# S5 output on TensorE as four 32-column sets side by side, with block 1's units and small steps in another order

## The reference, cut to what matters

```python
bu = jnp.einsum('blgh,gph->blgp', ug.astype(jnp.complex64), b_bar)
_, states = lax.associative_scan(combine, (a_seq, bu), axis=1)
y = jnp.einsum('blgp,ghp->blgh', states, c_mat).real + d.astype(f32) * ug
y = jax.nn.gelu(y.reshape(Bsz, L, S5_WIDTH))
y = y * jax.nn.sigmoid(y @ w_glu.astype(f32) + b_glu.astype(f32))
...
merged = g_s5 * (y_s5 @ w_br_s5[l]) + g_m * (y_m @ w_br_m[l])
x = x + merged @ w_out[l]
```

## Time and profile before

| | |
|---|---|
| median of 3 runs | 1433.69 us (1433.32 to 1433.8) |
| the profiled execution | 1439.07 us, of which the trace spans 1437.8 us |
| mean granted clock of TensorE | 0.949 of full speed |

### The profile page before, as it was taken

The page is one execution under the profiler, slowest core; times in us unless marked ns, Lnnn a source line. Parts: engine busy times, 40 slices in busy tenths (PEclk is TensorE's granted clock), DMA queues, the critical chain, the costliest instruction groups (busy, mean ns, idle before and its releaser), DMA issues. The chain is left out here.

```text
span 1437.8 us, 21155 instructions
## 1 busy us (share of the span) xinstructions
PE 1322.6 (92%) x8531; PEld 1204.6 (84%) x8537; DVE 897.0 (62%) x1291; ACT 590.5 (41%) x900; POOL 119.5 (8%) x152
## 2 busy tenths in 40 slices
PE   8988999999899999979987899999789898899996
PEld 5876788878589999869977799997779888799995
DVE  5957981125566777755476666666634585666666
ACT  2331111113355555543453554555411364554553
POOL 3890000003000000010000000010400000000000
PEclk9999899999999999999997999999887798999999
DMA  9434233427045556535502355565455202355561
GB/s 282 146 95 149 83 118 126 142 94 229 25 131 181 187 177 195 185 94 176 160 17 91 136 184 178 198 204 146 107 129 165 80 1 64 134 185 178 198 210 60
DMA packets 178590, 202.76 MB, mean 141 GB/s; under 512 B 21868, under 2 KB 163147, under 8 KB 178492
## 3 DMA queue, kind: packets, MB, share of 16 engines
q1 hardware_dynamic: 174939, 191.49, 42.0%
q0 software_dynamic: 3184, 9.77, 2.3%
q10 hardware_dynamic: 369, 0.13, 0.1%
HBM read 200.30 MB, written 1.08 MB: 140 GB/s over the span
## 5 line engine op out<-in xcount | busy, mean ns | idle before, releaser
L1317 DVE TENSOR_TENSOR w_parts<-raw,w_parts 128x1024 fp32r<-128x1024 f32 (+1 forms) x268 | 333.8, 1245 | 167.1 <-ACT w_parts L1306 159.6
L1306 ACT CAST w_parts<-raw 128x1024 fp32r<-128x1024 f32 (+1 forms) x268 | 279.3, 1042 | 337.6 <-PE ps L1600 103.3
L1600 PEld LDWEIGHTS ps<-hT_parts,w_parts 128*128 128x128 f32 x3024 | 366.6, 192 | 2.1
L1600 PE MATMUL ps<-hT_parts,w_parts 128*128 128x256 f32 x3024 | 367.6, 283 | 0.0
L1613 PE MATMUL ps<-w_parts,gT_parts 128*128 128x512 f32 x720 | 168.9, 390 | 0.0
L1613 PEld LDWEIGHTS ps<-w_parts,gT_parts 128*128 128x128 f32 x720 | 133.3, 188 | 26.4
L1366 PE MATMUL ps<-w_parts,hT_parts 128*128 128x256 f32 (+1 forms) x864 | 117.6, 303 | 16.7 <-DVE w_parts L1317 12.1
L1366 PEld LDWEIGHTS ps<-w_parts,hT_parts 128*128 128x128 f32 x864 | 116.2, 212 | 18.1 <-DVE w_parts L1317 12.5
L1364 PE MATMUL ps<-hT_parts,w_parts 128*128 128x256 f32 x912 | 120.8, 298 | 8.5 <-DVE w_parts L1317 4.5
L1364 PEld LDWEIGHTS ps<-hT_parts,w_parts 128*128 128x128 f32 x912 | 119.4, 207 | 10.0 <-issue 5.0
L451 PE MATMUL ps<-hT,ring 128*128 128x256 f32 x448 | 99.0, 380 | 1.0 <-DVE hT L310 1.0
(11 more groups left out here) (407 smaller groups left out, 1519.3 us busy)
## 6 DMA issues: line engine op xcount, KB each, us to landing
raw<-in_ffn_w_up SPq DMA_DIRECT2D x44, 1024.0 KB, 5.1
raw<-in_f_w_up SPq DMA_DIRECT2D x22, 1024.0 KB, 5.1
raw<-in_ffn_w_down SPq DMA_DIRECT2D x22, 1024.0 KB, 5.1
ring<-in_w_in SPq DMA_DIRECT2D x18, 1024.0 KB, 6.1
raw<-in_ev_w_in SPq DMA_DIRECT2D x15, 1024.0 KB, 5.4
raw<-in_f_w_down SPq DMA_DIRECT2D x11, 1024.0 KB, 4.9
ring<-in_x_wkv SPq DMA_DIRECT2D x8, 1024.0 KB, 5.5
ring<-in_w_out SPq DMA_DIRECT2D x4, 1024.0 KB, 5.1
```

The costliest lines, as they stand in the source:

```text
L1306: self.done(A, A.copy(high[:, c], self.raw[:, u % RAW, c]), self.s_hi)
L1317: self.done(V, V.tensor_tensor(low[:, c], self.raw[:, u % RAW, c], high[:, c].bitcast(F32), ALU.subtract), self.s_lo)
L1600: mm = T.matmul(self.ps[:, b, m * 256:m * 256 + 256], w[:, kk, m * P:(m + 1) * P], x[:, kk, :], start=kk == 0 and q == 0, stop=kk == KD - ...
```

## The change: what it does

1. `pe_s5_out` writes four tiles of 32 PSUM partitions in one bank. Pair m's weights are the 32 columns of `Cs` themselves at tile position (0, 32m). The products m = 0 to 3 use different columns of the array, and i = 1 (the imaginary part) adds to i = 0.
2. `CP` is gone, with its two clearings and 32 copies on DVE. PE waits for the scan's last addition (semaphore `x`) in place of the last copy (`cp`).
3. Units 8, 9 and 10 come one small step earlier: 8 ahead of the scores, 9 ahead of the turn, 10 ahead of the values, and no unit stands between the values and the first `pe_s5_in`.
4. The S5 steps and ym move among units 11 to 25, on PE and in step with it on ACT; on DVE the drain of ym moves from behind the second scan to behind the first.
5. The unit of `w_glu` becomes number 26 and the last values unit 27, and a unit of values stands between `w_glu` and the branch units.
6. Unit 32 no longer waits for the whole merged activation: its first half (j = 0) waits before each second k-block for the quarter that it reads.

```diff
@@ block1_memory
-        self.qkp, self.CP = p(18480, 8, SEQ + 3), [p(18480 + i * 512, 4, P) for i in range(2)]
+        self.qkp = p(18480, 8, SEQ + 3)
+        self.Cs = self.Bf
@@ early_units
-        u += [("T", wkv, D + c * 256, mT, KD, 256, 256) for c in range(4)]
+        values = [("T", wkv, D + c * 256, mT, KD, 256, 256) for c in range(4)]
+        u += values[0:3]
         u += [("F", I["s5_w_glu"][0], 0, self.yS, 4, 512, 256)]
+        u += values[3:4]
@@ pe_unit
-    def pe_unit(self, u):
+    def pe_unit(self, u, ready=None):
...
                 for kk in range(k):
+                    if ready is not None and j == 0 and kk % 2 == 0:
+                        T.wait_ge(*ready[kk // 2])
@@ pe_block1
-        T.wait_ge(*s5["merged"].at(4))
-        for u in range(32, 36):
+        self.pe_unit(32, [s5["merged"].at(i + 1) for i in range(4)])
+        for u in range(33, 36):
             self.pe_unit(u)
@@ pe_s5_out
-        T.wait_ge(*self.s5sem["cp"].next("T"))
+        T.wait_ge(*self.s5sem["x"].next("T"))
...
-                mm = T.matmul(self.ps[:, b, 0:256], self.CP[i][:, m, :], self.W5[5 + i][:, m, :],
-                              start=i == 0 and m == 0, stop=i == 1 and m == 3)
+                mm = T.matmul(self.ps[32 * m:32 * m + 32, b, 0:256], self.Cs[i][:, 4 * c4 + m, :], self.W5[5 + i][:, m, :],
+                              start=i == 0, stop=i == 1, tile_position=(0, 32 * m))
@@ act_block1 (the steps follow PE's order; the sigmoids of w_glu)
-        self.act_fill_unit(14)
         self.act_drain_gain(self.ym_fills, self.yM, "m_norm_g", kt=4)
+        self.act_fill_unit(14)
...
-            f = self.eu_fills[27][hh]
+            f = self.eu_fills[26][hh]
...
+        self.act_fill_unit(27)
@@ dve_block1
         self.dve_s5_scan(0)
+        self.dve_drain_gain(self.ym_fills, self.yM, "m_norm_g", kt=4)
         self.dve_s5_scan(1)
-        self.dve_drain_gain(self.ym_fills, self.yM, "m_norm_g", kt=4)
@@ dve_s5_scan
-            for i in range(2):
-                v1(v.memset(self.CP[i], 0.0))
...
-        v1(v.tensor_tensor(xi, xi, t1, ALU.add))
-        for i in range(2):
-            for m in range(4):
-                ins = v.tensor_copy(self.CP[i][:, m, 32 * m:32 * m + 32], self.Cs[i][:, 4 * c4 + m, :])
...
+        self.done(v, v.tensor_tensor(xi, xi, t1, ALU.add), s5["x"])
```

More of the change, by code:

```diff
@@ L495, in pe_block1 @@
         self.pe_mlstm_rows()
-        for u in (5, 6, 7):
+        for u in (5, 6, 7, 8):
             self.pe_unit(u)
         self.pe_mlstm_scores()
-        self.pe_unit(8)
+        self.pe_unit(9)
         self.pe_mlstm_turn()
@@ L502, in pe_block1 @@
         self.mem_fills = self.pe_transposes(self.MEM)
-        self.pe_unit(9)
+        self.pe_unit(10)
         self.pe_mlstm_values()
-        self.pe_unit(10)
         self.pe_wait_drained([self.eu_fills[5][0], self.eu_fills[6][0], self.bt_fills[1]])
         self.pe_s5_in(0)
-        self.pe_unit(11)
-        self.pe_unit(12)
+        for u in (11, 12, 13):
+            self.pe_unit(u)
         self.pe_s5_in(1)
-        self.pe_unit(13)
-        self.pe_s5_out(0)
-        self.pe_unit(14)
         T.wait_ge(*self.mls["h"].next("T"))
         self.ym_fills = self.pe_transposes(self.h8.rearrange("p (c h) d -> p c (h d)", c=2), kt=4)
+        self.pe_unit(14)
         self.pe_unit(15)
+        self.pe_s5_out(0)
+        self.pe_unit(16)
         self.pe_s5_in(2)
-        self.pe_unit(16)
-        self.pe_s5_out(1)
         self.pe_unit(17)
         self.pe_unit(18)
-        self.pe_s5_in(3)
+        self.pe_s5_out(1)
         self.pe_wait_drained(self.mem_fills[-2:])
         self.pe_unit(19)
+        self.pe_s5_in(3)
+        self.pe_unit(20)
+        self.pe_unit(21)
         self.pe_s5_out(2)
-        for u in (20, 21, 22):
+        for u in (22, 23, 24):
             self.pe_unit(u)
         self.pe_s5_out(3)
-        for u in range(23, 27):
-            self.pe_unit(u)
+        self.pe_unit(25)
         T.wait_ge(*s5["y"].at(4))
+        self.pe_unit(26)
         self.pe_unit(27)
@@ L694, in act_block1 @@
         self.act_fill_unit(8)
+        self.act_fill_unit(9)
         A.wait_ge(*self.full(self.st_fill))
@@ L697, in act_block1 @@
         self.act_drain_gain(self.mem_fills, self.memT, "mem_norm_g")
-        self.act_fill_unit(9)
+        self.act_fill_unit(10)
         A.wait_ge(*self.mls["num"].next("A"))
         self.done(A, A.activation(self.den, self.N[:, :, 128], ACT.Abs), self.mls["absden"])
-        self.act_fill_unit(10)
         self.act_root(self.ss_m)
@@ L704, in act_block1 @@
             self.act_fill_unit(u)
+        self.act_drain_gain(self.ym_fills, self.yM, "m_norm_g", kt=4)
         self.act_fill_unit(14)
-        self.act_drain_gain(self.ym_fills, self.yM, "m_norm_g", kt=4)
         self.act_fill_unit(15)
+        self.act_fill_unit(16)
         self.act_s5_gelu(0)
-        self.act_fill_unit(16)
-        self.act_fill_unit(17)
-        self.act_fill_unit(18)
+        for u in (17, 18, 19):
+            self.act_fill_unit(u)
         self.act_s5_gelu(1)
-        for u in (19, 20, 21):
+        for u in (20, 21, 22):
             self.act_fill_unit(u)
         self.act_s5_gelu(2)
-        for u in (22, 23, 24):
+        for u in (23, 24):
             self.act_fill_unit(u)
         self.act_s5_gelu(3)
-        for u in (25, 26):
-            self.act_fill_unit(u)
+        self.act_fill_unit(25)
         sg = self.sg
         for hh in range(2):
-            f = self.eu_fills[27][hh]
+            f = self.eu_fills[26][hh]
             A.wait_ge(*self.full(f))
-            bank = self.unit_bank(27, hh)
+            bank = self.unit_bank(26, hh)
             m = 2 * hh
@@ L751, in act_fill_unit @@
         else:
-            self.act_copy_unit(u, self.vX[:, :, (u - 23) * 256:(u - 22) * 256])
+            c = (23, 24, 25, 27).index(u)
+            self.act_copy_unit(u, self.vX[:, :, c * 256:(c + 1) * 256])
     def act_mlstm_decay(self):
@@ L827, in dve_block1 @@
             c = slice(2 * hh, 2 * hh + 2)
-            V.wait_ge(*self.drained(self.eu_fills[27][hh]))
+            V.wait_ge(*self.drained(self.eu_fills[26][hh]))
             self.done(V, V.tensor_tensor(self.yG[:, c, :], self.yS[:, c, :], sg[:, c, :], ALU.mult), s5["glu"])
-        V.wait_ge(*self.drained(self.eu_fills[26][0]))
+        V.wait_ge(*self.drained(self.eu_fills[18][0]))
         for u in (28, 29):
@@ L931, in dve_s5_c @@
         shp = [P, S5N, 32]
-        t0, t1, t2 = self.Bf[0], self.Bf[1], self.Ct
+        t0, t1, t2 = *self.Cs, self.Ct
         crb, cib = bc(self.cr, 2, shp), bc(self.ci, 2, shp)
@@ L940, in dve_s5_c @@
         v1(v.scalar_tensor_tensor(t1, t1, -1.0, t2, ALU.mult, ALU.subtract))
-        self.Cs = (t0, t1)
     def dve_s5_scan(self, c4):
@@ L1134, in block1 @@
         sem = self.sem
-        self.s5sem = {n: sem(f"s_s5_{n}") for n in ("ld", "w", "tab", "cn", "cp", "y", "glu", "merged")}
+        self.s5sem = {n: sem(f"s_s5_{n}") for n in ("ld", "w", "tab", "cn", "x", "y", "glu", "merged")}
         self.mls = {n: sem(f"s_mlstm_{n}") for n in ("g", "lse", "lf", "dg", "e", "eexp", "wst", "wexp", "conv", "silu", "num", "absden", "h")}
```

## The result

| | median | runs | ratio to before, with its 95% interval |
|---|---|---|---|
| before | 1433.74 us | 4 | |
| changed | 1404.25 us (1403.39 to 1404.47) | 4 | 0.9771 [0.9746, 0.9797] |
| before, another chip | 1433.43 us | 9 | |
| changed, that chip | 1400.08 us (1399.40 to 1401.47) | 4 | 0.9769 [0.9755, 0.9784] |

The change makes the kernel 29.5 us faster by the first medians and 33.3 by the second; the forecast was 32.2, 1401.5 us. The profiled execution of the changed kernel took 1404.47 us, of which the trace spans 1403.2. That is 34.6 us less than the span of the profiled execution before, and only 0.2 us above its own median, where the profiled execution before lay 5.4 above.

What follows compares the result with a forecast made beforehand. PE was taken to bound block 1, through its waits and the slow clock behind long ones. The terms 7.9 + 0.7 + 7.9 + 2.7 + 3.5 + 9.5 made 32.2 us, from 1433.7 to 1401.5 us, range 1398.5 to 1412.

Steps and rivals of the forecast that it cites:

- the first case: Whole kernel: all gains go as summed, 1399.5 to 1403.5 us, chance 0.65.
- a new wait or half an overlap: Rival: DVE margins too small or output steps of some 2 us, 1404 to 1409 us, chance 0.08.
- First stretch, 7.9: Block 1 up to the values: units 8 to 10 fill PE's waits and avoid the slow clock, 7.9 us gained.
- Middle, 0.7 + 7.9 + 2.7: Waits before the second pe_s5_in (0.7) and first pe_s5_out (7.9) go, and the latter's slow clock (2.7 us).
- End, 3.5: End of block 1: waits before the branch units (1.93) and w_out (1.58) are covered, 3.5 us gained.
- Output steps, 9.5: Four pe_s5_out steps fall from 3.45 to 1.08 us each with column tiles, 9.5 us gained.
- the row tiles' price: Output step priced like pe_s5_in, 16 instructions in four row tiles: 1.08 us from start to start.
- The rival of sets that don't overlap: Output steps keep 3.45 us because column sets don't overlap: 1411.0 us, chance 0.18.
- the slower one: Tiled float32 instructions run singly at the low clock in the output steps, as high as 1446.7 us: chance 0.02.
- Margins on DVE: DVE ready ahead of PE by 4.8 us at the second pe_s5_in and 5 us at the first pe_s5_out.
- What follows block 1: Stages after block 1 follow PE's last units and move as a whole, with no length change in the sum.
- given back later: Rival: clock changes in later stages cost part of the gain, 1403 to 1408 us or as much lower, chance 0.07.

Runs made afterwards that it cites:

- e1: The kernel before, run again without an edit for a second profile: 1434.59 us, ratio 0.9996 to before.
- e5: The changed kernel, run again without an edit on a second chip: 1400.08 us, ratio 0.9769 to before.
- e6: The changed kernel with units 8, 9 and 10 back at their old places: 1411.15 us, ratio 0.9842 to before.
- e3: The kernel before with the new order alone, keeping CP, its clearings and copies and the full-array output step: 1412.29 us, ratio 0.9832 to before.
- e7: The changed kernel with w_glu's unit last before the branch units and unit 32 waiting for the whole merged activation: 1410.11 us, ratio 0.9838 to before.
- e4: The kernel before with 34 products of zeros on PE ahead of the first output step: 1434.22 us, ratio 0.9985 to before.
- e11: The changed kernel with w_glu's unit and unit 32's wait as before, measured once more on a third chip: 1408.16 us, ratio 0.9814 to before.
- e9: The kernel before with the column tiles alone, plus 22 products of zeros ahead of the first output step: 1420.84 us, ratio 0.9897 to before.
- e2: The kernel before with the column tiles alone, CP gone, in the old order: 1429.30 us, ratio 0.9948 to before.

## Why the prediction was right

The sum was right for the part that it was made for: 32.2 us against 32.3 in the two traces (225.2 less 192.9) and 31.7 between e1 and e5. That the first median, 1404.25, came so near to 1401.5 is in part luck, for the step from the trace to the median was wrong. The forecast took the 5.4 us by which the profiled execution lay above the median to be the same after the change. They were 0.2: the profiled time was forecast as 1406.9 and came at 1404.47, 2.4 us lower, the median came 2.8 us higher. With 1404.25 the result also lies 0.75 us outside the 1399.5 to 1403.5 of the first case, where the ranges of two rivals begin; e5's 1400.08 lies inside. The traces rule out the first of these rivals, a new wait or half an overlap. The mean clocks were 0.954 to 0.955 in the first measurement and 0.956 to 0.960 in e5; by the slope above the difference makes 3.5 of the 4.2 us between the two.

The parts, by the traces:

- **First stretch, 7.9.** e6 gives 7.9. Of its two halves, waits and slow clock, the second is no fixed amount: 3.15 us in the trace of before (scores and unit 8), 1.6 in e1, and there behind another wait. The waits are 5.28 and 5.68. From unit 7 to the values the traces of before take 35.3 and 34.4 us, those of the changed kernel 34.5 and 33.6 with a unit of 6.95 more: the edit is worth 6.9 to 8.7. That full clock in the scores alone is worth little follows from e1 and e6: PE then waits for DVE's product at the turn, the bound that I had used for what is left and not for what stands before.
- **Middle, 0.7 + 7.9 + 2.7.** All three are gone, by the timeline; no run puts them back alone. What e3, e6 and e7 leave of the 31.7 us between e1 and e5 is 31.7 less 9.0, 7.9 and 3.9, or 10.9, where the three terms make 11.3. The third was 2.7 in one trace and 2.1 in the other; e4 shows by itself that it comes from the idle time.
- **End, 3.5.** In the trace of e7 the waits are 3.5. The medians of e7 and e11 make it 6.5 to 10. If the medians are right, this is the term that was mis-sized: I counted a slower clock behind the long waits only.
- **Output steps, 9.5.** 9.0. The choice of the row tiles' price was right: 1.01 us a step against 1.08. The rival of sets that don't overlap and the slower one fall with it. By the 2.38 of the Trainium skill (TensorE: Matmul & The Clock Gate, Part 3), given there for three tiles, the estimate for a step was 1.45 us; here four sets gave 3.4 times. About 0.1 us is lost on either side of a tiled step in the comparison with e3. I had counted it as nothing; it is 0.8 us of the sum. The Trainium skill (TensorEngine Tiling (Array Packing), Key Properties) states that a change of the tiling mode drains the engine; the 0.1 us fits that, and no run here tells a drain from another cause.
- **Margins on DVE.** 4.8 and 5 us were forecast, 4.0 and 4.3 measured (`pe_s5_in(1)` at 128.25 against banks free at 124.24).
- **What follows block 1.** The forecast had it move as a whole, but its own length varies from 1137.4 to 1144.6 us between traces of identical code, and it divides by the order in block 1: the six traces in the old order have 1142.9 to 1144.6, the eight in the new one 1137.4 to 1141.3, 4.3 us less in the mean. So in the traces nothing is given back later, the rest is even shorter. In e1, e4 and e9 the clock from 850 to 950 us behind the start of `w_out` is 0.83, in e5 0.90; before and e2 lose 3.1 us against e5 in the first 122 us behind it, at a clock of 0.97 for 1.00 over 125 us in before. Whether the earlier end of block 1 brings this or the choice of the profiled executions does (before, e1, e4 and e9 were above their medians), no run shows. The distance ahead of unit 7 scatters as well, 67.5 and 69.0 us in the two traces of the changed kernel.

## What to carry to other kernels

Products with 32 output columns each needed no zero padding here: four sets of them side by side took 1.01 us where the padded ones took 3.46, and DVE, which had to build the padded weights, is relieved as well. Ask of a slow clock behind a wait whether removing it alone brings anything: another engine may be due just behind it, and the slow clock may then stand behind that wait. An idle time of PE can cost more than it lasts, even one of 2 us. But don't trust a sum from one trace when executions scatter with the clock, nor carry the distance between profiled time and median from one kernel to the next: compare stretches inside the traces, and whole times over many runs.

## What the runs showed of the hardware

The instructions of the output step in the changed kernel, by their own view (weight loads, then products; ns shortest/median/longest), and the weight loads of the step before the change:

```profile
L593 PEld LDWEIGHTS ps<-arena x64: 106/110/110, 144.2 to 212.9; 128*32 128x32 f32 x64
L593 PE MATMUL ps<-arena x64: 379/379/403, 144.2 to 213.2; 128*32 128x256 f32 x64
...
L585 PEld LDWEIGHTS ps<-arena x64: 190/190/337, 146.4 to 228.1; 128*128 128x128 f32 x64
```

A product takes as long by itself as one on the full array, a median of 379 ns, and 16 of them with four different sets of columns pass in 1.01 us; a weight load of 32 columns takes 110 ns where one of 128 takes 190.

I had not expected that a wait of 1.93 us could be followed by the lower clock. In four of the eight traces it was, with the same loss of 1.7 us each time, in the other four not at all. Behind a wait of 2.9 us at the turn the clock was 0.51 over 3.46 us in e1 and 0.56 over 3.22 us in e6.
